# Three terms outside, eight feature tiles inside: the order of the projection matmuls on TensorE

## What is computed

```
z = rmsnorm(x, g_norm) @ w_in                  # 1024 -> 3328 columns: q, k, v, gates, conv inputs
o = windowed attention of q, k, v with sinks   # 8 heads of 64, window 128
mix = concat(o * silu(ga), bg * conv3(cg * hc) * silu(gc))
x = x + mix @ w_out                            # 1024 -> 1024
x = x + sigmoid(x @ w_pg) * (p @ w_pp)         # 1024 -> 1024 and 256 -> 1024
```

## Time and profile before

| | |
|---|---|
| median of 3 runs | 1144.07 us (1143.65 to 1144.09) |
| the profiled execution | 1144.57 us, span 1142.5 us |
| TensorE, matmuls | 1133.7 us busy, 99% of the span, 7255 matmuls |
| TensorE, weight loads | 1120.1 us, 98%, 7255 loads |
| VectorE, ScalarE, GpSimdE | 674.0, 495.7 and 501.0 us busy |
| DMA | 71.53 MB, mean 63 GB/s |

### The profile page before, as it was taken

How to read it: one execution, slowest core, us unless ns; L and a number is a source line. 1 busy time by engine, 2 the same in 40 slices (tenths; PEclk the granted TensorE clock), 3 DMA queues, 4 the chain that set the end, 5 groups by cost and what they waited for, 6 DMA issues and landing times.

```text
span 1142.5 us, 18780 instructions
## 1 busy us (share of the span) xinstructions
PE 1133.7 (99%) x7255; PEld 1120.1 (98%) x7255; DVE 674.0 (59%) x1233; ACT 495.7 (43%) x1126; POOL 501.0 (44%) x655
## 2 busy tenths in 40 slices
PE   8999999999999999999999999999999999999998
PEld 8999999999999999999999999999999999999998
DVE  3175878888844444555614476879786444444435
ACT  6312656666643222333322146575755322133335
POOL 4493456666652232222446344566666323222220
PEclk9999999999999999999999999999999999999999
DMA  8741111111112212111074211111111212211104
GB/s 240 197 111 38 37 38 37 38 38 38 38 38 77 60 47 62 48 46 43 20 199 116 58 38 38 38 38 38 37 38 38 68 51 57 65 46 47 46 1 153
DMA packets 126820, 71.53 MB, mean 63 GB/s; under 512 B 41224, under 2 KB 121960, under 8 KB 126700
## 3 DMA queue, kind: packets, MB, share of 16 engines
q1 hardware_dynamic: 124408, 63.70, 19.7%
q10 hardware_dynamic: 2324, 6.64, 2.5%
HBM read 60.18 MB, written 6.77 MB: 59 GB/s over the span
## 4 chain that ended last, share of the span: by engine, by line
PE 89%; DVE 6%; ACT 3%; issue 1%; DMA 1%; SPq 0%; DVEq 0%
PE ring L507 82%; PE aux L521 2%; PE aux L545 2%; PE aux L530 1%; DVE yc L1340 1%; DMA xnat<-in_x_prompt_dram 1%; DVE st L1205 1%; DVE kst L1236 1%; ACT ptcp L879 1%; DVE qst L1233 0%; DVE up L1336 0%; DVE comb L1203 0%; DVE raw L1253 0%; PE aux L594 0%; PE aux L619 0%
## 5 line engine op out<-in xcount | busy, mean ns | idle before, releaser
L507 PE MATMUL ring<-act,ws 128*128 128x352 f32 (+2 forms) x6048 | 1000.4, 323 | 0.0
L507 PEld LDWEIGHTS ring<-act,ws 128*128 128x128 f32 x6048 | 967.2, 188 | 3.4
L488 POOL TENSOR_TENSOR ws<-stage,ws 128x256 fp32r<-128x256 f32 x352 | 283.8, 838 | 495.7 <-ACT ws L808 494.9
L482 POOL TENSOR_TENSOR stage<-stage,gT 128x256 f32<-128x256 f32 x208 | 143.9, 721 | 31.8 <-DMA stage<-in_w_in_dram 31.8
L817 ACT ACTIVATE act<-tmp 128x352 fp32r<-128x352 f32 x120 | 59.6, 496 | 223.1 <-DVE tmp L1380 143.6
L808 ACT ACTIVATE ws<-stage 128x1024 fp32r<-128x1024 f32 (+1 forms) x83 | 90.5, 1090 | 40.9 <-PE ring L507 17.9
L1102 DVE TENSOR_TENSOR act<-tmp,act 128x352 fp32r<-128x352 f32 x120 | 74.7, 623 | 40.2 <-ACT act L817 40.0
L461 POOL TENSOR_SCALAR_AFFINE_SELECT pw<-pw 128x512 fp32r<-128x512 f32 x56 | 38.6, 692 | 74.4 <-ACT pw L967 67.4
L1378 DVE TENSOR_TENSOR tmp<-ring,act 128x352 f32<-128x352 f32 x48 | 25.2, 524 | 66.9 <-PE ring L507 66.9
L507 PE MATMUL ring<-pT,ws 128*128 128x352 f32 (+2 forms) x288 | 53.9, 322 | 0.0
L956 ACT ACTIVATE gate<-gate 128x352 f32<-128x352 f32 x48 | 23.8, 497 | 65.0 <-DVE gate L1285 40.3
(11 more groups left out here) (199 smaller groups left out, 1006.1 us busy)
## 6 DMA issues: line engine op xcount, KB each, us to landing
stage<-in_w_in_dram SPq DMA_DIRECT2D x36, 512.0 KB, 3.9
stage<-in_w_in_dram SPq DMA_DIRECT2D x32, 256.0 KB, 3.8
stage<-in_w_pg_dram SPq DMA_DIRECT2D x16, 512.0 KB, 3.8
rotq<-raw ACTq DMA_DIRECT2D x32, 132.0 KB, 2.4
xnat<-in_x_prompt_dram SPq DMA_DIRECT2D x8, 512.0 KB, 7.9
stage<-in_w_out_dram SPq DMA_DIRECT2D x32, 128.0 KB, 2.9
stage<-in_w_out_dram SPq DMA_DIRECT2D x16, 256.0 KB, 3.1
ptcp<-in_p_prompt_dram SPq DMA_DIRECT2D x4, 512.0 KB, 4.7
```

Source lines behind the costliest of these rows:

```text
L482: scaled = nc.gpsimd.tensor_tensor(part, part, gT[:, l, k:k + 2].rearrange("p (k a) -> p k a", a=1) .to_broadcast([P, 2, P]), ALU.mult)
L488: rest = nc.gpsimd.tensor_tensor(ws[:, s, 1, k:k + 2, :], stage[:, s, k:k + 2, :], ws[:, s, 0, k:k + 2, :].bitcast(F32), ALU.subtract)
L507: mm = nc.tensor.matmul(out, ws[:, w % 2, wp, kw, :], x[:, xp, kx, cs], start=(i == 0 and wp == 0 and xp == 0), stop=(i == n - 1 and wp == 1))
```

## The change

The loop over the three terms becomes the outer one, the loop over feature tiles the inner one. A group now makes high by high for all eight tiles, then high weights by low x for all eight, then low weights by high x for all eight. The work of `inside` keeps its place: what stood ahead of tile i, so ahead of matmul 3i, still stands ahead of matmul 3i. The waits for tiles all stand in the first term, at matmuls 0 to 7.

```
-                for i, (kw, kx) in enumerate(tiles):
-                    if inside and i in inside:
-                        inside[i]()
-                    if waits:
-                        pe.wait_ge(*waits(i))
-                    for wp, xp in ((0, 0), (0, 1), (1, 0)):
+                for term, (wp, xp) in enumerate(((0, 0), (0, 1), (1, 0))):
+                    for i, (kw, kx) in enumerate(tiles):
+                        if inside and (term * n + i) % 3 == 0 and (term * n + i) // 3 in inside:
+                            inside[(term * n + i) // 3]()
+                        if waits and term == 0:
+                            pe.wait_ge(*waits(i))
                         mm = nc.tensor.matmul(out, ws[:, w % 2, wp, kw, :], x[:, xp, kx, cs],
-                                              start=(i == 0 and wp == 0 and xp == 0), stop=(i == n - 1 and wp == 1))
+                                              start=(term == 0 and i == 0), stop=(term == 2 and i == n - 1))
                 mm.then_inc(group_done, 1)
```

## The result

The changed kernel takes 1153.53 us (median of 4 runs, 1153.20 to 1154.12) against 1144.08 us for the kernel before on the same chip (4 runs, 1143.65 to 1144.79): ratio 1.0082, 95% interval 1.0067 to 1.0097. It is slower by 9.45 us; the forecast was no change, and the time lies above the range. The span grew by 8.8 us, from 1142.5 to 1151.3 us.

A forecast was written before the change was run, and what follows sets the result against it. TensorE's back-to-back matmuls, without waits, were taken to bound the kernel. Profiled 1144.57 + 0 + 0 + 0 = 1144.6 us; the runs' median is 0.5 us lower, so 1144.0 us, range 1134 to 1150 us.

The forecast's parts named there:

- the first of the change's three parts: New neighbours of each projection matmul: 21 of 23 steps in a group go to the next tile; cost 0, bounds ±12.4 us.
- the kind of step: Whether successive projection matmuls keep the weights, change them, or go to the next feature tile; taken to cost 0.
- The rival of steps that settle higher: 352-column projection steps settle at 160.0 ns (at most +5.6 us, 1149.7 us) or 161.2 (1156.5 us); chance 0.22.
- The rival of steps that settle lower: 352-column projection steps settle one notch lower, 157.9 ns (-6.2 us, 1137.9 us), or two (1131.7 us); chance 0.30.
- the 14 ns that do not go with the columns: About 14 ns of each 352-column projection step, independent of column count; the only portion the change could touch.
- The second part: Semaphore waits for tiles in 15 groups come up to 2.2 us earlier; least cover left 3.7 us, cost 0.
- The third part: Work put between matmuls stays at the same matmul count, weight and bank waits at the group's start; cost 0.
- the marks set for a wrong prediction: Stretches at 158 ns, or 160 and more (span moves about 5.6 us per ns), or a line 1102 wait in 15 groups.

The follow-up runs named there:

- order 4 of the first run: One of six orders alternating by output tile in one kernel (1147.04 us, one run): terms outside, tiles 0 2 1 3 4 6 5 7 inside; settles at 160.0 ns.

## Why the prediction was wrong

The step that failed is the first of the change's three parts: "I take 0 for the kind of step." The kind of step that the new order multiplies was judged from seven starts rounded to 10 ns, and 2.8 ns, the difference from 158.9 to 161.7 in the settled step, is below that rounding. What the seven starts could show, that no load is saved or added, was right: the counts are equal, and the runs with even and odd tiles apart never keep weights in a group of eight tiles and lose at most 0.2%. By the rule of the Trainium skill ("TensorE: Matmul & The Clock Gate", Part 2, loading the stationary operand) the parting of equal weights would be the loss; the run with the low half moved keeps every pair of equal weights and loses as much (0.87% against 0.82%), so the trace does not bear that out here.

The rival of steps that settle higher named the right thing, that x's address moves by one tile at each matmul, though not that its residue counts. Its two prices, 1149.7 us at 160.0 ns and 1156.5 us at 161.2, stand on either side of the 1153.53 us measured; it was given 0.22, and the range took in only the lower. Both go by steps of the old order. The new pattern has values of its own, 161.7 and 158.3 ns, and 172 of 195 groups take the upper one. Priced at 161.7 against a mean of (149 x 158.9 + 34 x 160.0 + 12 x 161.1) / 195 = 159.2, 5616 x 2.5 = 14.0 us would have been too much: in stage A many groups are interrupted or settle at 158.3, and it loses 2.4 of 1872 x 2.5 = 4.7 us.

The rival of steps that settle lower named 157.9 ns; 158.3 does occur, in 23 groups, too few to matter. That it was given more chance than the higher one rested on a single step that rounds to 0.15 us and on the 14 ns that do not go with the columns. These 14 ns come from 288 and 352 columns alone: from 352 to 384 the same rows give 175.5 - 159.0 = 16.5 ns for 32 columns, 0.52 each, and 352 columns of 0.52 ns would be more than the whole step.

The second part held: all waits were covered. The tile for stage C of layer 2 in the changed kernel:

```profile
1017.45 0.53 DVE L1102 TENSOR_TENSOR act<-tmp,act 128x352 fp32r<-128x352 f32 x1 [0.57 <-ACT act L817]
```

It is there at 1017.98 us and wanted at 1020.53 + 7 x 0.175 = 1021.76 us, so 3.8 us are left, as forecast. The third part held too: no wait of TensorE on weights or banks appeared. Of the marks set for a wrong prediction the first came true, with the sign of "160 ns and more"; the scale given there, about 5.6 us for each ns, is too steep: stage B's 2.1 ns would be 11.8 us, and 8.1 us were measured.

What stays open: why the addresses matter, that is, what in the reading of x and the weights makes a pattern of residues settle at these values, and what in an interruption chooses between 158.3 and 161.7 ns, beyond the residue with which a group begins. A layout in which every tile starts at a multiple of 256 bytes was not tried (the two buffers of x would need 4096 bytes more), nor were the weights moved with one residue for all of x.

## What to carry to other kernels

Where matmuls run back to back without a wait, the order of equal work is not free: look at the start addresses of successive moving operands and of the weights that they run with, and read the step from start to start over long uninterrupted stretches, since 2 ns in 160 are 1% of the kernel. A row of rounded starts can exclude a cost of tens of ns, not one of two. Before an order is judged, move one operand by 128 bytes with the order kept: that tells an address effect from one of the order.

## What was not expected of the hardware

At 352 columns the step takes few exact values in most of these runs, and which ones goes with the pattern of x's residues of 256 bytes against that of the weights: with the weights at 128 past a multiple, 158.3 with all tiles at a multiple of 256, 160.0 with all at 128 past it (some groups of either kind stand at 161.1 to 166.7), 158.9, 160.0 or 161.1 where the residue changes every third matmul (the order before), 160.0 in pairs (order 4 of the first run), 158.3 or 161.7 in strict turns (the changed order). At 384 columns it is 173.3 ns with one residue, 175.5 in the order before and 175.0 in turns; at 288 it is 131.7 with one residue and 133.3 in either order. With even and odd tiles apart, moving the weights by 128 bytes made the values of the two residues change places. An identical stream can hold either of two values for over a hundred matmuls. "TensorE: Matmul & The Clock Gate" of the Trainium skill (Part 2, the back-to-back issue gap) gives N / 2.4 + 2.5 ns for isolated matmuls, by which an estimate for 352 columns is 149 ns; the measured steps of 158.3 to 161.7 ns, each with its own load of weights, lie 9 to 13 ns above that.
